# Feed-forward input of a transformer layer: the three weight sums of each seven-product block on GpSimd

## What is computed

```python
h = rms_norm(x, ffn_pre_g[l])                      # 256 x 2048
gate, up = jnp.split(h @ w_ffn_in[l], 2, axis=-1)  # w_ffn_in: 2048 x 11264
x = x + rms_norm((jax.nn.silu(gate) * up) @ w_ffn_out[l], ffn_post_g[l])
```

## Time and profile before

| | us |
|---|---|
| median of 2 executions (2426.61 to 2428.27) | 2427.44 |
| the profiled execution | 2427.59 |
| its span, first to last instruction | 2425.3 |
| TensorE busy | 2406.8 (99%) |
| VectorE busy | 1673.4 (69%) |
| ScalarE busy | 1304.1 (54%) |
| GpSimd busy | 36.9 (2%) |

### The profile page before, as it was taken

How to read it: one execution, slowest core, us unless ns; L and a number is a source line. 1 busy time by engine, 2 the same in 40 slices (tenths; PEclk the granted TensorE clock), 3 DMA queues, 4 the chain that set the end, 5 groups by cost and what they waited for, 6 DMA issues and landing times.

```text
span 2425.3 us, 33378 instructions
## 1 busy us (share of the span) xinstructions
PE 2406.8 (99%) x12195; PEld 2008.9 (83%) x12195; DVE 1673.4 (69%) x2305; ACT 1304.1 (54%) x1813; POOL 36.9 (2%) x60
## 2 busy tenths in 40 slices
PE   9999999999999999999999999999999999999998
PEld 7888888897888888888887889998788888888887
DVE  5568888677888888864446536777788888884444
ACT  5665558665555555544445435554655555554443
POOL 1000000000000000000000010000000000000000
PEclk9999999999999999999999999999999999999999
DMA  7765545545556555666656775435565565656554
GB/s 236 241 207 187 161 149 176 165 158 170 178 191 223 190 193 182 199 223 195 194 192 204 218 223 157 145 109 157 159 203 192 190 216 190 196 194 214 193 191 156
DMA packets 233853, 455.82 MB, mean 188 GB/s; under 512 B 16698, under 2 KB 19002, under 8 KB 233232
## 3 DMA queue, kind: packets, MB, share of 16 engines
q1 hardware_dynamic: 227008, 431.49, 55.6%
q0 software_dynamic: 6160, 21.81, 2.6%
q10 hardware_dynamic: 576, 1.05, 0.1%
HBM read 449.04 MB, written 5.24 MB: 187 GB/s over the span
## 4 chain that ended last, share of the span: by engine, by line
PE 93%; DVE 3%; ACT 1%; DMA 1%; issue 1%; DVEq 0%; SPq 0%; ACTq 0%
PE g L320 12%; PE g L321 12%; PE g L322 12%; PE g L1173 9%; PE g L1175 9%; PE g L1174 9%; PE g L1577 4%; PE g L1579 4%; PE g L1578 4%; PE m L1136 1%; PE m L1138 1%; PE m L1137 1%; PE g L2514 1%; PE g L2518 1%; PE g L2516 1%; PE g L1136 1%
## 5 line engine op out<-in xcount | busy, mean ns | idle before, releaser
L308 DVE TENSOR_TENSOR wl<-raw,wh 128x1024 fp32r<-128x1024 f32 (+1 forms) x820 | 991.0, 1219 | 591.4 <-ACT wh L304 578.2
L304 ACT ACTIVATE wh<-raw 128x1024 fp32r<-128x1024 f32 (+1 forms) x819 | 858.5, 1055 | 867.2 <-PE g L322 395.3
L1173 PE MATMUL g<-wh,act_hi 128*128 128x512 f32 x960 | 374.8, 390 | 0.4 <-DVE shared L1355 0.4
L1175 PE MATMUL g<-wh,act_lo 128*128 128x512 f32 x960 | 373.5, 389 | 0.0
L1174 PE MATMUL g<-wl,act_hi 128*128 128x512 f32 x960 | 373.5, 389 | 0.0
L320 PE MATMUL g<-wh,ht_hi 128*128 128x512 f32 x672 | 261.6, 389 | 0.0
L322 PE MATMUL g<-wh,ht_lo 128*128 128x512 f32 x672 | 261.4, 389 | 0.0
L321 PE MATMUL g<-wl,ht_hi 128*128 128x512 f32 x672 | 261.4, 389 | 0.0
L1173 PEld LDWEIGHTS g<-wh,act_hi 128*128 128x128 f32 x960 | 180.2, 188 | 38.5 <-issue 0.8
L1175 PEld LDWEIGHTS g<-wh,act_lo 128*128 128x128 f32 x960 | 180.2, 188 | 37.7
L1174 PEld LDWEIGHTS g<-wl,act_hi 128*128 128x128 f32 x960 | 180.2, 188 | 37.2
(11 more groups left out here) (476 smaller groups left out, 3550.9 us busy)
## 6 DMA issues: line engine op xcount, KB each, us to landing
raw<-in_w_ffn_in SPq DMA_DIRECT2D x176, 512.0 KB, 4.4
raw<-in_ffn_w_in SPq DMA_DIRECT2D x176, 512.0 KB, 4.4
raw<-in_w_in SPq DMA_DIRECT2D x111, 512.0 KB, 4.5
raw<-in_w_ffn_out SPq DMA_DIRECT2D x88, 512.0 KB, 4.4
raw<-in_ffn_w_out SPq DMA_DIRECT2D x88, 512.0 KB, 3.8
raw<-in_nsa_w_in SPq DMA_DIRECT2D x80, 512.0 KB, 4.4
raw<-in_w_out SPq DMA_DIRECT2D x32, 512.0 KB, 4.4
raw<-in_nsa_w_out SPq DMA_DIRECT2D x32, 512.0 KB, 4.8
```

What stands on the lines that cost most here:

```text
L304: nc.scalar.activation(wh[:, j % SLOTS, 0:n], raw[:, j % SLOTS, 0:n], ACT.Copy).then_inc(hi_done, 1)
L308: nc.vector.tensor_tensor(wl[:, j % SLOTS, 0:n], raw[:, j % SLOTS, 0:n], wh[:, j % SLOTS, 0:n].bitcast(F32), ALU.subtract).then_inc(lo_don ...
L1173: nc.tensor.matmul(dst, h, whk, start=(t in starts and k == 0), stop=False)
L1175: ins = nc.tensor.matmul(dst, l, whk, start=False, stop=(last and k == 1))
```

## The change

`weight_sums` leaves VectorE's program. GpSimd gets a loop of its own over the ten passes of each layer, with the same three adds for each block, the same operands and the same order. The signal between its second and third add was a step of `ff_step`; now the second add and the third raise `raw_full` of the fourth unit's slot by 8 each, 16 together as before. The numbering of `ff_step` shrinks from 6 to 4 steps a pass. `half_unit` on VectorE gets a wait: it makes the low part of the block's second unit, whose signal lets SyncE load over that unit, only when GpSimd's second add has read it.

```diff
-        STEPS = {"t2": (1, 3), "rows": 2, "u2": 4, "u34": 5, "shared": 6}
+        STEPS = {"rows": 1, "u2": 2, "u34": 3, "shared": 4}
...
-            return LAYER[name] * (6 * (PAIRS - 1) + 1) + 6 * (i - 1) + step
+            return LAYER[name] * (4 * (PAIRS - 1) + 1) + 4 * (i - 1) + step
...
-            def weight_sums(i, p):
...
-                nc.vector.tensor_tensor(halves[:, t3:t1 + 1, :], halves[:, b12:b12 + 1, :].broadcast_to([P, 2, NB]),
-                                        halves[:, b22:b21:b21 - 1 - b22, :], ALU.add).then_inc(raw_full[(j + 2) % SLOTS], 16)
-                dve.wait_ge(raw_full[(j + 2) % SLOTS], (cyc + (j + 2) // SLOTS) * 16 + 16)
-                nc.vector.tensor_tensor(halves[:, t2, :], halves[:, t1, :], halves[:, b22, :], ALU.add).then_inc(ff_step, 1)
-                dve.wait_ge(ff_step, ff_stepped(name, i, STEPS["t2"][p]))
-                nc.vector.tensor_tensor(halves[:, t4, :], halves[:, t2, :], halves[:, b21, :], ALU.add)\
-                  .then_inc(raw_full[(j + 3) % SLOTS], 16)
...
             def half_unit(i, j):
                 cyc = ff_cyc(s, i)
                 dve.wait_ge(hi_done, (cyc + j // SLOTS) * SLOTS + j % SLOTS + 1)
+                dve.wait_ge(raw_full[(j + 2) % SLOTS], (cyc + (j + 2) // SLOTS) * 16 + 8)
...
                 for j in range(FF_NEXT):
-                    if j in SEVEN_AT:
-                        weight_sums(i, SEVEN_AT.index(j))
                     if j in SEVEN_AT:
                         ahead_unit(i, j)
...
+        def pool_ffn_in(pool, name):
+            s = gemms[name]
+            halves = raw[:, :, :].rearrange("p s (k n) -> p (s k) n", k=2)
...
+            def weight_sums(i, p):
+                cyc, j = ff_cyc(s, i), SEVEN_AT[p]
+                s1, s2, s3 = ((j + q) % SLOTS for q in range(1, 4))
+                b21, b12, b22, t3, t1, t2, t4 = 2 * SLOTS + 1, 2 * s1, 2 * s1 + 1, 2 * s2, 2 * s2 + 1, 2 * s3, 2 * s3 + 1
+                pool.wait_ge(ahead_in, ahead_no(name, i, p))
+                pool.wait_ge(raw_full[s1], (cyc + (j + 1) // SLOTS) * 16 + 16)
+                pool.wait_ge(lo_done, SLOTS + (cyc + (j - 1) // SLOTS) * SLOTS + (j - 1) % SLOTS + 1)
+                nc.gpsimd.tensor_tensor(halves[:, t3:t1 + 1, :], halves[:, b12:b12 + 1, :].broadcast_to([P, 2, NB]),
+                                        halves[:, b22:b21:b21 - 1 - b22, :], ALU.add).then_inc(raw_full[s2], 16)
+                pool.wait_ge(raw_full[s2], (cyc + (j + 2) // SLOTS) * 16 + 16)
+                nc.gpsimd.tensor_tensor(halves[:, t2, :], halves[:, t1, :], halves[:, b22, :], ALU.add).then_inc(raw_full[s3], 8)
+                pool.wait_ge(raw_full[s3], (cyc + (j + 3) // SLOTS) * 16 + 8)
+                nc.gpsimd.tensor_tensor(halves[:, t4, :], halves[:, t2, :], halves[:, b21, :], ALU.add).then_inc(raw_full[s3], 8)
+
+            with pool.Fori(1, PAIRS) as i:
+                for p in range(SEVENS):
+                    weight_sums(i, p)
...
+            pool_ffn_in(pool, "ff1")
             pool.wait_ge(ff_step, ff_stepped("ff1", PAIRS, 1))
...
+            pool_ffn_in(pool, "ff2")
             pool.wait_ge(lo_evac, BANKS["ff2"] + 2 * PAIRS)
```

## The result

The changed kernel takes 2466.89 us (median of 2 runs, 2461.35 to 2472.43) against 2427.44: a ratio of 1.0164, 95% interval 1.0132 to 1.0196. Measured again (e12), the same kernel took 2459.49 us (median of 4, 2451.12 to 2461.55), ratio 1.0119 (1.0103 to 1.0135). Against the kernel before, measured beside it each time, it is slower by 32 to 39 us, outside the range that was given (2425 to 2440). Its times scatter over 21 us, those of the kernel before over less than 6. The profiled execution took 2461.35 us, its span is 2459.6.

The account below looks back on a forecast made before the run. TensorE was taken to bound the kernel, so moving VectorE's sums gains nothing by itself: 2427.59 us profiled minus 0.2 for first-pass holes is 2427.4, by the median 2427.3 us; range 2425 to 2440.

Parts of the forecast that it names:

- What bounds the kernel: TensorE is full in the steady loop; only the first passes have holes, 2.2 us; relieving VectorE gains nothing by itself.
- about 2% from no change: What this kernel's measurement was said to be able to tell apart; a result of "same" got chance 0.95.
- The price of the adds: On GpSimd 2.16 us for the wide add, 1.08 for each short one, 4.5 us a block with hand-overs.
- no visible change: Main forecast: the moved sums come in time in both blocks of a pass; 2426.5 to 2428.5 us, chance 0.57.
- rival 1: GpSimd and VectorE cannot read SBUF together; first blocks' up_rows late by 0.1 to 0.4 us; about 2431 us, chance 0.27.
- is covered: Under rival 1 the second unit's load lands at 800.2 instead of 798.4, still before TensorE wants it at 804.3.
- Rival 2: GpSimd's chain outlasts the block's lead at the second block's fourth unit, beyond 7.0 us; 2451 us, chance 0.10.
- The wait in half_unit: In first blocks VectorE's new wait for the second sum ends at 792.8, before rounding at 793.04; costs nothing.
- What the profile would show: VectorE busy near 1569 us, GpSimd adds of 2.2 and 1.1 us, TensorE's two-pass stretch still 85.7; signs for each rival.

Follow-up runs that it names:

- e12: The changed kernel measured again, nothing else altered, against the kernel before: 2459.49 us, ratio 1.0119.
- e8: Kernel before, sums still on VectorE, with the low part of the block's first unit ahead of the sums and up_rows ahead of unit 3's low part: 2424.08 us.
- e13: Changed kernel with each sum replaced by two GpSimd fills that read no input, chain 5.2 us, the sums' undisturbed length: 2427.05 us, ratio 1.0002.
- e6: Kernel before with only the second block's sums of each pass (units 9 to 12) moved to GpSimd: 2438.90 us, ratio 1.0040.
- e9: Changed kernel with each sum replaced by GpSimd fills that read no input, lengthened to a chain of 6.2 us: 2451.05 us, ratio 1.0099.
- e1: Changed kernel with half_unit's wait for GpSimd's second sum moved to SyncE, ahead of the load that overwrites the second unit: 2449.27 us, ratio 1.0095.
- e10: Changed kernel with up_rows placed ahead of unit 3's low part on VectorE: 2451.15 us, ratio 1.0099.
- e14: Changed kernel with up_rows ahead of unit 3's low part and the wait for the second sum on SyncE instead of VectorE: 2449.36 us, ratio 1.0099.
- e2: Kernel before, sums on VectorE, with GpSimd making three adds of the same sizes on spare data in each block: 2571.34 us, ratio 1.0593.

## Why the prediction was wrong

**What bounds the kernel** was right: a full TensorE, holes of 2.2 us, nothing to gain from an unburdened VectorE. e8 gained 3.3 us, with an interval of 1 to 5 us, which fits the 2.2 that there were. The sentence that the measurement tells about 2% from no change was too careful: the intervals here are 0.1 to 0.3% to each side, and a loss of 1.2 to 1.6%, "same" by the 2% mark, stands clear of them.

**The price of the adds** was off by a tenth for the wide one and a fifth for the short ones (2.39 and 1.29 for 2.16 and 1.08), and this didn't matter: e13 has the true length and loses nothing. The forecast "no visible change" was thus right for a GpSimd that excludes nobody.

**The step that failed** is rival 1's sum, and the choice against it. The mechanism was named there, with its place and its order in turns; it was given a chance of 0.27 and a price of 4 us, 2 to 8. Measured are 32 to 39. At the one deadline that it priced, up_rows in the first blocks, it was right: the waits there rose from 1.5 to 7.1 us. Three things were missing.

First, the second blocks lose as well, which the sum had declared safe (e6: 11.5 us). For the block that it was made from, the sum was near: in the one that TensorE starts at 816.39 the third unit's low part ended 1.3 us into the block, where the sum gives 1.5, and nobody waited. But the lead isn't the same in every block. After the change ten of the 20 second blocks had a lead of 5.0 us or less, and TensorE waited inside all ten; the other ten had 5.5 and more, and it waited in none.

Secondly, every block was computed from the leads of the profile of before, as if each began afresh. Low parts that end late give slots back late, and the load that the next block's sums wait for lands later: the lead in the second layer's second blocks fell from 6.0 to 4.5 us on the mean, to 3.2 at the worst. The sentence that this delay of the loads "is covered" was true for the one load that I followed and not for that one.

Thirdly, the shared sums of unit 15 and their wait (7.1 us of TensorE's) don't occur in the prediction at all; they stand in VectorE's queue behind the second block's low parts.

**Rival 2's break-even** was 7.0 us for the chain, and e9 loses 23 at 6.2. The place was right: of some 19 us that TensorE waits inside e9's blocks, 15.5 are in second blocks, and 10.5 of these at the fourth unit. The lead was wrong. It was taken as the 6.0 us of the earlier trace rows, which gave 7.0; by the same sum a chain of 6.2 needs a lead of 5.2. In the profile of before the 20 second blocks have leads from 3.9 to 6.5 us, and three are under 5.2 already; in e9 thirteen are, with 4.6 on the mean of the 20, and these thirteen are the ones in which TensorE waits. (In e13 the mean stays at 5.9.) So the cliff is nearer than the one block shows, at first by the spread that one could have read before, and then because a longer chain shortens the lead of later blocks: the load ahead of the sums took 5.6 us in e9, 4.4 before and in e13.

**The wait in half_unit** I had at no cost. Alone it is (e13); beside the exclusion, taking it off VectorE gave 10 to 17 us back (e1), but nothing that shows where up_rows already stood early (e10 and e14, both 1.0099). Why it costs there I can only argue: it puts the half low part behind the second add, and with it the low parts and up_rows that follow.

**What the profile would show** was right for rival 1: low parts that begin to move only when an add ends, adds longer than alone, L1136 waiting for up_rows. But rival 2's signs are there too, ScalarE's L304 waiting for GpSimd (68 us, where e13 has 14.5 at no cost) and TensorE for L308 (8.7 us): the exclusion makes the chain long, and so both rivals come true together, which the prediction had as alternatives. VectorE's 1569 us became 1632.

## What to carry to other kernels

Before work is moved between VectorE and GpSimd, count VectorE's two-input operations beside it: each add on GpSimd that reads SBUF is time taken from both, and 2.6 us a block on VectorE became 6.3 us on GpSimd, with VectorE's own operations held up beside them. A deadline computed from the leads of the old profile holds only if the change delays nothing that feeds the lead; in this ring of four slots the delay came back as a late load (5.5 us from issue to landing for 4.4). And a deadline is checked against the shortest lead of the old profile, not against one block's. Where the bound engine is full, look for its few holes in order, not in load: two changes of order gave 3 us here.

## What the runs showed of the hardware

A fill on GpSimd (128x2048 in 1.82 us) runs beside a two-input operation of VectorE at no cost to either; an add doesn't. An operation of VectorE with one of its two inputs in PSUM (up_rows) runs beside an add at its own length (e10). That two engines without any dependence could cost 144 us (e2) I had not expected. There the granted clock also fell: 0.94 in the stretch 781.9 to 867.6, where TensorE was busy for 76.93 of 85.70 us, and 0.983 over the span, against 0.999 before. In the two loops it stood at half, the 1.2 GHz level, for 82 us in 18 stretches. One of them came just after TensorE had stood idle for 3.47 us ahead of the matmul at 848.77; there the matmuls start 0.43 us apart in place of 0.227. By the starts of all matmuls the steps with a wait ahead of them grew by 103 us and the others by 41, half of the 82: so of the 144 us some 100 are waits and some 40 the clock. Byte-wise fills took 1.81 us for 2048 bytes a partition and 0.96 for 1024, about as much an element as fp32 fills (0.53 us for 512).
